# Weighing two expert slots at once in four 64x64 quarters of TensorE's array

## What is computed

```
def block(ub):                                   # 128 tokens
    q  = (ub @ wq).reshape(tb, 8, 2, 128)        # 8 heads, two halves
    s1 = einsum('thd,hnd->thn', q[:, :, 0], sub_keys[:, 0])
    s2 = einsum('thd,hnd->thn', q[:, :, 1], sub_keys[:, 1])
    t1, i1 = top_k(s1, 16);  t2, i2 = top_k(s2, 16)
    cand = t1[..., :, None] + t2[..., None, :]   # 256 candidates
    top, pos = top_k(cand, 16)                   # 16 experts a head
    g   = softmax(top)
    act = gelu(einsum('td,tkd->tk', ub, up[eidx]))
    return einsum('tk,tkd->td', g * act, down[eidx])
x = layer_norm(alpha * x + g2 * block(x * (1 + sc2) + sh2))
```

## Time and profile before

| | |
|---|---|
| timed runs | 4849.0, 4858.26, 4859.0 us, median 4858.26 |
| profiled execution | span 4851.8 us from the first to the last instruction; the profile gives no other time of it, and the timed runs lie within 0.2% of the span |
| busy over the span | TensorE matmul 4056.9 us (84%), VectorE 3217.5 (66%), GpSimd 1502.4 (31%), ScalarE 843.4 (17%) |
| moved by DMA | 1484.23 MB, of which 1342.26 MB by the gathers of the expert stage (1280 of them) |
| weighing, L723 | 5120 passes, 2433.3 us |
| mean granted clock of TensorE | 0.952 |

### The profile page before, as it was taken

One profiled execution on the slowest core, in us unless ns is written; L12 is line 12 of the kernel. 1 busy time (PEld: TensorE's weight loads), 2 busy tenths in 40 slices (PEclk: granted clock), 3 DMA queues, 4 the chain that ended last, 5 costly groups with the idle time before them and its releaser, 6 DMA issues.

```text
span 4851.8 us, 47489 instructions
## 1 busy us (share of the span) xinstructions
PE 4056.9 (84%) x11304; PEld 1920.3 (40%) x11304; DVE 3217.5 (66%) x8492; ACT 843.4 (17%) x2182; POOL 1502.4 (31%) x1349
## 2 busy tenths in 40 slices
PE   8999899687887887887888879989788788788887
PEld 1354675333333333333333324456433333333332
DVE  0220864787777887787787863065588787778776
ACT  0100341111111111111111111023111111111111
POOL 0000010344443443443444430001144344344443
PEclk9999799999999999999999999989899999999999
DMA  9411112999998998998999982122499899899998
GB/s 325 161 52 50 66 63 77 365 416 404 376 417 364 420 414 341 411 418 337 420 418 385 416 334 72 38 98 83 170 411 419 343 414 413 335 418 416 391 412 355
DMA packets 260491, 1484.23 MB, mean 306 GB/s; under 512 B 23943, under 2 KB 48775, under 8 KB 95767
## 3 DMA queue, kind: packets, MB, share of 16 engines
q0 software_dynamic: 184320, 1342.26, 67.3%
q1 hardware_dynamic: 76060, 140.67, 8.5%
HBM read 1476.40 MB, written 2.24 MB: 305 GB/s over the span
## 4 chain that ended last, share of the span: by engine, by line
PE 51%; DVE 26%; issue 15%; DMA 6%; DVEq 2%; ACT 1%; POOL 0%; SPq 0%; POOLq 0%; ACTq 0%
PE ps L723 22%; PE ps L715 6%; DMA arena<-in_updown,arena 5%; PE ps L565 4%; DVE arena L1312 3%; DVE arena L1305 3%; PE ps L522 3%; PE ps L580 3%; PE ps L683 3%; PE ps L585 2%; DVE arena L1275 1%; PE ps L652 1%; DVE arena L1280 1%; DVE arena L1278 1%; PE ps L608 1%
## 5 line engine op out<-in xcount | busy, mean ns | idle before, releaser
L723 PE MATMUL ps<-arena 128*128 128x512 f32 x5120 | 2433.3, 620 | 537.8 <-DVE arena L1305 534.7
L976 POOL DMA_INDIRECT arena<-in_updown,arena x1280 | 1461.4, 1142 | 2225.6 <-PE ps L723 1717.8
L723 PEld LDWEIGHTS ps<-arena 128*128 128x128 f32 x5120 | 938.2, 194 | 2000.5 <-DVE arena L1305 1157.6
L1312 DVE CUSTOM_DVE_ANT_0 arena<-arena 128x1024 bf16<-128x1024 f32 x1280 | 1563.2, 1221 | 173.5 <-DMA arena<-in_updown,arena 107.5
L920 ACT ACTIVATE arena<-arena 128x1 f32<-128x1 f32 x1280 | 252.2, 202 | 2726.3 <-DVE arena L1312 2688.5
L1305 DVE TENSOR_SCALAR arena<-CN,arena 128x128 f32<-128x128 f32 x1280 | 440.9, 344 | 85.6 <-ACT arena L920 46.7
L963 POOL TENSOR_TENSOR arena<-arena 128x256 f32<-128x256 f32 x64 | 40.7, 667 | 1092.9 <-DMA arena<-in_bias 1092.9
L715 PE MATMUL ps<-arena 128*128 (+1 forms) x1280 | 302.4, 391 | 2.3 <-ACT arena L936 2.3
L1237 DVE MAX8 arena<-ps 128x8 f32<-128x128 f32 x80 | 24.0, 299 | 388.4 <-PE ps L715 388.2
L715 PEld LDWEIGHTS ps<-arena 128*128 128x128 f32 x1280 | 252.7, 198 | 68.5 <-issue 32.5
L565 PE MATMUL ps<-arena 128*128 128x512 f32 (+1 forms) x672 | 233.5, 508 | 0.0
(11 more groups left out here) (184 smaller groups left out, 2894.6 us busy)
## 6 DMA issues: line engine op xcount, KB each, us to landing
arena<-in_ada_w SPq DMA_DIRECT2D x24, 2048.0 KB, 7.9
arena<-in_updown,arena POOLq DMA_INDIRECT x1280
arena<-in_wq SPq DMA_DIRECT2D x32, 512.0 KB, 4.3
arena<-in_w_in SPq DMA_DIRECT2D x6, 2048.0 KB, 8.8
arena<-in_w_in SPq DMA_DIRECT2D x24, 512.0 KB, 3.8
arena<-in_bias SPq DMA_DIRECT2D x16, 512.0 KB, 3.6
arena<-in_w_out SPq DMA_DIRECT2D x2, 4096.0 KB, 13.4
arena<-negm_rows SPq DMA_DIRECT2D x16, 384.0 KB, 4.4
```

Source lines behind the costliest of these rows:

```text
L723: mm = e.matmul(ps[hf][:], diag[:, k % 2, :], ring[:, k % RING, D + hf * 512:D + (hf + 1) * 512], start=False, stop=False, skip_group_chec ...
L976: e.indirect_dma_start(ring[:, k % RING, :], None, updown, bass.IndirectOffsetOnAxis(ap=idx16[:, k:k + 1], axis=0)).then_inc(sem(f"rows{k ...
L1312: e.tensor_tensor_reduce(prod[:, k % 2, :], ring[:, k % RING, 0:D], u, 1.0, 0.0, ALU.mult, ALU.add, dots[:, k:k + 1]).then_inc(sem("L.dot_ ...
```

## The change

Two neighbouring slots are weighed at once. The diagonal is no longer 128x128 but 128x64: `id64` holds, in each row p, a one in column p modulo 64, so that rows 0 to 63 and rows 64 to 127 each hold a 64x64 diagonal. For a pair of slots TensorE does eight matmuls of 64 rows by 64 columns. For slot `s` of the pair and row half `g` the input rows are those of half `g`, and the output goes to partitions of half `(g + s) % 2` in bank `2g + hf`. So the four products of one `hf` lie in the four quarters of the array, and the accumulators are four banks instead of two. The sum of the even slots of tokens in half `g` lies in the same half of bank `2g + hf`, that of the odd slots in the other half.

At the end of the tile both must be added, and they lie on different partitions: ScalarE copies the parts on the foreign half into a new buffer `other`, and VectorE adds the own half of each bank to it, in four operations, and multiplies with the gate in one more. There are four closing and four opening matmuls. The semaphore `L.slot_done` becomes `L.pair_done`, GpSimd waits once for two gathers, and there are four diagonals instead of two. The banks of the key scores and the turned tokens move up by two.

```
-        diag = r(2, P)
+        HALF = P // 2
+        diag = r(4, HALF)
+        id64 = r(HALF)
...
-                def weigh(n, k):
-
-                    e.wait_ge(sem("L.diag_ready"), n + (k + 1))
+                def weigh_pair(n, k):
+
+                    e.wait_ge(sem("L.diag_ready"), n + (k + 2))
+                    e.sem_inc(sem("pe_token"), 1)
                     for hf in range(2):
-                        mm = e.matmul(ps[hf][:], diag[:, k % 2, :], ring[:, k % RING, D + hf * 512:D + (hf + 1) * 512],
-                                      start=False, stop=False, skip_group_check=True)
-                    mm.then_inc(sem("L.slot_done"), 1)
+                        for s in range(2):
+                            for g in range(2):
+                                rows, to = slice(g * HALF, (g + 1) * HALF), (g + s) % 2 * HALF
+                                mm = e.matmul(ps[2 * g + hf][to:to + HALF, :], diag[rows, (k + s) % 4, :],
+                                              ring[rows, (k + s) % RING, D + hf * 512:D + (hf + 1) * 512],
+                                              start=False, stop=False, skip_group_check=True)
+                    mm.then_inc(sem("L.pair_done"), 1)
...
-                    for hf in range(2):
-                        mm = e.matmul(ps[hf][:], zero, ln2r[:, 0, 0:512], start=False, stop=True, skip_group_check=True)
+                    for b in range(4):
+                        mm = e.matmul(ps[b][:], zero, ln2r[:, 0, 0:512], start=False, stop=True, skip_group_check=True)
                     mm.then_inc(sem("L.acc_ready"), 1)
...
+                    e.wait_ge(sem("L.acc_ready"), t + 1)
+                    e.sem_inc(sem("act_token"), 1)
+                    e.wait_ge(sem("L.other_free"), t + 1)
+                    e.sem_inc(sem("act_token"), 1)
+                    for g in range(2):
+                        at, to = (1 - g) * HALF, g * HALF
+                        for hf in range(2):
+                            ins = e.activation(other[to:to + HALF, hf * 512:(hf + 1) * 512], ps[2 * g + hf][at:at + HALF, :], ACT.Copy)
+                    ins.then_inc(sem("L.other_ready"), 1)
                     e.wait_ge(sem("L.var2"), t + 1)
...
-                        e.wait_ge(sem("L.slot_done"), un * TOPK + (k + 1))
-                        e.sem_inc(sem("pool_token"), 1)
+                        if k % 2 == 0:
+                            e.wait_ge(sem("L.pair_done"), un * (TOPK // 2) + (k // 2 + 1))
+                            e.sem_inc(sem("pool_token"), 1)
...
                         e.wait_ge(sem("L.act_done"), un * UN + (k + 1))
-                        e.wait_ge(sem("L.slot_done"), un * UN + (k - 1 + RING))
-                        e.tensor_scalar(diag[:, k % 2, :], ident, acts[:, k:k + 1], gate_all[:, bass.ds(un * UN + k, 1)], ALU.mult, ALU.mult).then_inc(sem("L.diag_ready"), 1)
+                        if k % 2 == 0:
+                            e.wait_ge(sem("L.pair_done"), un * (UN // 2) + (k // 2 - 1 + RING // 2))
+                        e.tensor_scalar(diag[:, k % 4, :], id64, acts[:, k:k + 1], gate_all[:, bass.ds(un * UN + k, 1)], ALU.mult, ALU.mult).then_inc(sem("L.diag_ready"), 1)
...
-                        for hf in range(2):
-                            c = slice(hf * 512, (hf + 1) * 512)
-                            ins = e.tensor_tensor(junk[:, c], ps[hf][:], g2r[:, c], ALU.mult)
+                        e.wait_ge(sem("L.other_ready"), t + 1)
+                        e.sem_inc(sem("dve_token"), 1)
+                        for g in range(2):
+                            own = slice(g * HALF, (g + 1) * HALF)
+                            for hf in range(2):
+                                c = slice(hf * 512, (hf + 1) * 512)
+                                ins = e.tensor_tensor(junk[own, c], ps[2 * g + hf][own, :], other[own, c], ALU.add)
                         ins.then_inc(sem("L.acc_free"), 1)
                         e.wait_ge(sem("L.acc_free"), t + 2)
+                        lc.link(e.tensor_tensor(junk, junk, g2r, ALU.mult))
+                        e.sem_inc(sem("L.other_free"), 1)
```

More of the change, by code:

```diff
@@ L213, in build @@
         epsc = sb("epsc", [P, 1])
-        ARENA_W = 45900
+        ARENA_W = 46000
         arena = sb("arena", [P, ARENA_W])
@@ L347, in build @@
         sd2 = r(2)
+        other = r(D)
         ring = r(RING, 2 * D)
+        assert RING % 2 == 0
         keys = Region(keys_at)(2 * PH, NKEY)
@@ L712, in key_scores @@
                         e.wait_ge(sem("L.route_read"), unit + 2 - lead)
-                    bank = ps[2 + (unit % 2 if lead == 2 else 0)]
+                    bank = ps[4 + (unit % 2 if lead == 2 else 0)]
                     for k in range(KD):
@@ L734, in tile @@
                         key_scores(t * PH + h + LEAD, h + LEAD, 1)
-                        for k in range(TOPK):
-                            weigh(t * (PH * TOPK) + h * TOPK, k)
+                        for k in range(0, TOPK, 2):
+                            weigh_pair(t * (PH * TOPK) + h * TOPK, k)
                     if more:
@@ L1230, in _, with route @@
                     UN = TOPK
-                    def route(un, bank=2):
+                    def route(un, bank=4):
                         e.wait_ge(sem("L.key_mm"), un + 1)
@@ L1375, in _ @@
                         lc.restart()
-                        for _ in route(h, 2 + h % 2):
+                        for _ in route(h, 4 + h % 2):
                             pass
```

20 lines of the change are left out of this document (11 added, 9 removed).

## The result

The changed kernel takes 5159.54 us, the median of four runs (5153.33 to 5167.05), against 4856.27 us for the kernel before (4849.0 to 4859.0). The ratio is 1.0629 with a 95% interval of 1.0614 to 1.0644. It is 303 us slower, where 37 were forecast. The direction was right and the time far outside the range.

A forecast was written before the change was run, and what follows sets the result against it. The prediction saw an engine ring bounding units, with DMA's 39.8 us floor 0.3 us behind. Per tile -2.4 (body) +5.1 (hand-over) +1.0 (clock) = +3.7 us, ten tiles +37: 4895 us, own range 4862 to 4945, 8 in 10 range 4862 to 4965.

The forecast's parts named there:

- What bounds the kernel: Expert stages: an engine ring at 40.08 us a unit, with a DMA floor of 39.8 us right behind it.
- the ring of engines: Mid-tile unit: VectorE and TensorE wait on each other, 40.08 us a unit; the change would close this in 37.3 us.
- Weighing: TensorE's matmuls for a pair of slots: from 3.4 us to 1.7 to 2.2 us with quarters side by side.
- column case: Rival for weighing: column halves run in turn, a pair takes 3.4 us, 4960 us in all; chance 0.16.
- Release by pairs: Giving ring places back two at once: costs nothing in mid-tile, with 2.5 us of cover left; 2.4 us after a hand-over.
- body of a tile: First key-score search to slot 15 of the tile's last unit: -3.3 to -1.4 us, taken as -2.4.
- 0.5 lost while pairs come slower than they are fetched: Term in the tile body's sum after the change: 0.5 us, within a total of 309.0 us.
- Hand-over: Slot 15's dot product to the next tile's first search: +5.1 us a tile, uncovered, plus 1.0 for the clock.
- Clock: TensorE's granted clock falls to 0.72 in expert stages: covered in mid-tile by the DMA floor, +1.0 us at the hand-over.
- the clock decides: Rival: at 1.2 GHz pair and key scores end 5.2 us later, about +27 us a tile, 5125 us; clock chance 0.11.
- Faster: Rival: DMA not at its limit, units close in 37.3 us, -13.5 us a tile, 4723 us; chance 0.06.
- no quarters side by side: Rival for weighing: a pair takes 6.8 us, units 58 us, over 6200 us in all; chance 0.02.

The follow-up runs named there:

- before_late_search_2: Kernel before, with VectorE's top-k search begun after slot 2's dot product instead of slot 0's: 4790.04 us, ratio 0.9867.
- pairs_full_array: Kernel before with its full-array 128x128 matmuls, but slots weighed and places released in pairs; no quarters, no gathering: 5289.53 us, ratio 1.0885.
- ring_seven: Kernel before, but GpSimd waits for one slot more before refilling, so seven of the ring's eight places are in use: 4993.64 us, ratio 1.0285.
- changed_kept_busy: Changed kernel with filler matmuls by zeros into an unused bank in TensorE's idle time: 5012.24 us, ratio 1.0323.
- changed_late_search: Changed kernel, with VectorE's top-k search begun after slot 2's dot product instead of slot 0's: 4868.55 us, ratio 1.0034.
- changed_by_slot: Changed kernel with its diagonals, banks and gathering, but each slot weighed and given back alone: 4871.36 us, ratio 1.0040.
- quarters_by_slot: Kernel before with four quarters filled from one slot, column halves holding the halves of D, each slot released alone: 4850.83 us, ratio 0.9992.

## Why the prediction was wrong

**What bounds the kernel: right as to the floor.** I had two limits 0.3 us apart, the ring of engines and DMA's 39.8 us. before_late_search_2 reached 39.76 us. Whether the 0.3 us above it came from the ring or from late refills no run separates, since the later search takes away both.

**Weighing: right.** A pair was taken at 1.7 to 2.2 us and takes 1.95 at the full clock, 3.69 at half. The column case is refuted: 16 passes one after the other by column halves would take 3.4 us. The Trainium skill, "TensorEngine Tiling (Array Packing)", section Key Properties, says that tiles work independently of one another; the 1.95 us agree with that, for four quarters in float32.

**Release by pairs: this is the step that failed.** It said that the fetch of slot 8 "must begin about 11.7 us after L1237", that an issue at 7.5 becomes traffic 1.6 us later, and: "2.5 us of cover are left. It costs nothing there". The traces show the queue running out from about 8 us on and the first issue at 9.3. Three terms were mis-sized.

1. *When the requests run out.* I worked back from slot 15's dot product at 32.3 us, since I took 7.5 us from there to the next search. In the kernel before it is 31.1, and in the changed one the stretch from slot 15 to the search was 8.3 us in the median and not 7.5 (9.4 and 10.9 in the two units above). With 31.1 the 11.7 come 1.2 us earlier.
2. *A slot lands with the slowest of 16 DMA engines.* I allowed 0.7 us from landing to dot product and nothing for the spread between the engines. The kernel before shows the spread where the last gather of its first layer ends: windows first, then the last dot product.

```profile
2884.00:2886.00 2.00, 1.50 (x4) 0.49 (x3) 1.10 (x3) 0.20 (x1) 0.00 (x0) 1.00 0.96 401
2886.00:2888.00 2.00, 1.50 (x4) 0.49 (x3) 1.49 (x3) 0.20 (x1) 0.00 (x0) 1.00 0.18 74
```

```profile
2888.55 1.23 DVE L1312 CUSTOM_DVE_ANT_0 arena<-arena 128x1024 bf16<-128x1024 f32 x1 [0.97 <-DMA arena<-in_updown,arena]
```

From 2886 on little more is fetched, yet the last slot comes at 2888.55. Its 16 landings run from 2886.12 to 2888.53, 2.4 us: 15 of them are in by 2887.43, and one engine comes 1.1 us later. These rows were there to be read before the result. In mid-tile the spread is smaller, 1.5 us in the median before and 1.8 in the changed kernel, there mostly between 1.1 and 2.5. The Trainium skill, "DMA: Bandwidth & Descriptors", section "Why a DMA increments its semaphore by 16 and not by 1", says that the engines finish independently and that all 16 must have counted. This case's trace agrees, with 2.4 us between the first and the last at that place.

3. *When the first issue comes.* Forecast 7.5, measured 9.3. Most of it is the first pair at half clock (3.69 instead of 1.95 us), 1.7 us; I had priced the low clock at the end of a unit and not there.

Put together, with 2.5 us taken for the spread: 11.7 - 1.2 - 2.5 = 8.0 us until the queue is empty. Averaged over the mid-tile units, the rate stays above 410 GB/s until 8 us after the search, in the changed kernel and in pairs_full_array, and then falls: to 209 between 8 and 9 us with pairs on the full array, to 217 between 9 and 10 in the changed kernel. A first issue at time x makes traffic at x + 1.6, so by this estimate DMA stands still for x + 1.6 - 8.0. For the changed kernel that is 2.9 us (measured: units 3.3 longer), for pairs_full_array 5.1 (5.8), for ring_seven 1.2 (1.9), for changed_kept_busy 1.2 (1.2), and for the kernel before -0.8, the cover it had in the average unit. In ring_seven both times are those of the slot ahead, 2.5 us earlier, which leaves the difference as it is.

The sum comes within 0.7 us of the growth of a unit, but the growth does not all lie where the sum puts it. The bytes that a unit's traffic stays short of 422 GB/s, as time, in the 56 units that follow another and precede one in their tile:

| us short in a unit | 5 to 16 us after the search | later |
|---|---|---|
| before | 0.3 | 0.3 |
| changed | 2.2 | 1.6 |
| pairs_full_array | 5.8 | 0.5 |
| ring_seven | 1.7 | 0.7 |
| changed_kept_busy | 0.5 | 1.2 |
| changed_late_search | 0.0 | 0.2 |

So for pairs_full_array and ring_seven the sum is borne out. In the changed kernel the first gap is 1.9 us longer than before and not 2.9, and in changed_kept_busy, where the sum seems exact, the loss lies mostly elsewhere: that agreement is chance. What is shown is that the loss in both places goes when the first release comes early (changed_late_search) or slot by slot (changed_by_slot, 0.1 us short in all). How the 3.7 us divide between the first two terms is only worked out; no run separates them, and with the spread of mid-tile they would be about 3.

So the "body of a tile" was forecast at -2.4 us and came to +25.8. "0.5 lost while pairs come slower than they are fetched" stood in that sum; it was lost in all eight units and many times over.

**Hand-over: right.** Forecast +5.1 and +1.0 for the clock, measured +4.9 each and +6.0 at the end.

**Clock: right in level, wrong in effect.** I took 0.72 for the stage; the slices show mostly 7 and 8 tenths, the span 0.827. That its price lay "within the 2.5 us that the DMA floor leaves" fails with the cover. By changed_kept_busy the clock carries 147 of the 303 us where the first release is late; in changed_late_search, as low at 0.836 and with the same passes, units are at the floor. The rival "the clock decides" named 5125 us, near the measured 5159.54, but by another mechanism: key scores and last pair late at the end of a unit. The changed kernel's own trace refutes that, since its key scores take 3.72 us in the median against 3.62 before; so does changed_late_search, as cold and at the floor. That 5125 came near is luck: a number that lies near does not show its mechanism. The Trainium skill, "TensorE: Matmul & The Clock Gate", Part 1, says that the engine is gated down unless kept busy. The traces agree (0.952 before, 0.827 with TensorE busy 67% instead of 84% of the span); what it cost here depended on who waited for the cold pass.

**Rivals.** Faster, and no quarters side by side: refuted. None of the rivals held the one that came true, a ring that runs dry in every unit, since I had costed it at nothing in the body of the text.

**What stays open.** In the changed kernel 1.6 us of the 3.9 that a unit is short of the DMA's full rate fall later than 16 us after the search, in dips down to 297 GB/s between 19 and 29 us. They go with the late first release, but no run shows how they arise, or how much of the clock's 147 us is lost in them.

## What to carry to other kernels

When work on a buffer is batched, ask first when the buffers come free, not how fast the batch runs: here two slots at once freed the first place of a unit one slot later and behind a wait of another engine, and a ring with some 0.8 us to spare lost 3.3 us in each unit. Size the cover of such a ring by when the DMA queue empties (its rate in short windows, with the last slot's wait beside it), and not by when the consumer needs the data. And where a stage is bound by DMA, look for the wait that delays the next request before making any engine faster: starting the search behind slot 2 brought 65 us, the quarters nothing.

## What the runs showed of the hardware

- Four 64x64 quarters work side by side in float32: 16 passes of 64x512 in 1.95 us at the full clock and 3.69 at half. Four passes on the full array take 1.7 us (0.43 each), so the four quarters cost a seventh more than perfect overlap.
- The 16 DMA engines do not end a gather together: between the first and the last landing of one slot lie 1.5 us in the median in mid-tile of the kernel before, 1.8 in the changed kernel, and 2.4 at the end of the first layer before.
- In quarters_by_slot, with the four quarters working at once, a mean granted clock of 0.785 over the span went with the same time as 0.952 before (ratio 0.9982 to 1.0003).
- Two PSUM copies of 128x512 on ScalarE took 1.09 us, four of 64x512 took 2.16: half the partitions save no time.
